# An encoder layer with experts on one core: rows of the first two experts taken from the residual by selection products

## What is computed

```
x = x + concat(a, b) @ w_out                      # residual after attention
t = rmsnorm(x, ffn_norm)
gl = t @ router_group + bias                       # 4 groups, the best is taken
el = t @ router_expert + bias                      # 8 experts in it, the best two are taken
out = sum over experts e: gates[:, e] * ((silu(t @ w_gate[e]) * (t @ w_up[e])) @ w_down[e])
y = rmsnorm(x + out, final_norm)
```

## Time and profile before

| | us |
|---|---|
| runs, median of 3 | 815.48 (814.65 to 816.72) |
| the profiled execution | 814.7 |
| its span, first to last instruction | 812.9 |
| mean granted clock of TensorE | 0.963 of full |
| TensorE busy | 711.2 (87%) |
| VectorE, ScalarE, GpSimd busy | 322.4, 214.0, 201.1 |
| hardware queue, software queue | 138.20 MB, 15.75 MB |

### The profile page before, as it was taken

The page is one execution under the profiler, slowest core; times in us unless marked ns, Lnnn a source line. Parts: engine busy times, 40 slices in busy tenths (PEclk is TensorE's granted clock), DMA queues, the critical chain, the costliest instruction groups (busy, mean ns, idle before and its releaser), DMA issues. The chain is left out here.

```text
span 812.9 us, 12172 instructions
## 1 busy us (share of the span) xinstructions
PE 711.2 (87%) x3978; PEld 399.4 (49%) x3979; DVE 322.4 (40%) x900; ACT 214.0 (26%) x575; POOL 201.1 (25%) x478
## 2 busy tenths in 40 slices
PE   6899999999988999989999965999997899999910
PEld 3455544444355666665555544555443445555500
DVE  3863121110088888881555561211111112111138
ACT  2433210011177777771211111111110111111123
POOL 1224232220024231132001223532232334342110
PEclk9999999999999999999999986999999999999975
DMA  8703002000140000000891168999999979999856
GB/s 299 295 1 104 0 1 103 1 0 1 35 178 1 1 1 1 2 2 0 344 418 69 76 238 307 303 336 378 396 343 386 355 258 365 407 374 394 356 224 254
DMA packets 40823, 154.64 MB, mean 190 GB/s; under 512 B 9642, under 2 KB 10794, under 8 KB 31936
## 3 DMA queue, kind: packets, MB, share of 16 engines
q1 hardware_dynamic: 33120, 138.20, 45.2%
q0 software_dynamic: 7648, 15.75, 5.8%
HBM read 142.29 MB, written 20.03 MB: 200 GB/s over the span
## 5 line engine op out<-in xcount | busy, mean ns | idle before, releaser
L1397 PE MATMUL banks<-arena 128*128 128x512 f32 (+1 forms) x384 | 163.4, 579 | 10.2 <-DMA arena<-w_in 8.0
L1662 PE MATMUL banks<-arena 128*64 128x256 f32 x1280 | 150.2, 388 | 10.6 <-DVE arena L1343 6.3
L1662 PEld LDWEIGHTS banks<-arena 128*64 128x64 f32 x1280 | 92.2, 139 | 59.4 <-issue 11.7
L1397 PEld LDWEIGHTS banks<-arena 128*128 128x128 f32 x384 | 72.1, 193 | 85.6 <-issue 77.9
L1553 PE MATMUL banks<-arena 128*128 128x512 f32 x192 | 86.4, 598 | 1.1 <-DVE arena L1162 1.1
L1672 PE MATMUL banks<-arena 128*64 128x512 f32 x320 | 77.4, 605 | 3.5 <-DVE arena L1347 3.1
L1118 DVE TENSOR_REDUCE arena<-banks 128x1 f32<-128x512 f32 (+1 forms) x96 | 55.3, 599 | 49.3 <-PE banks L1469 41.9
L904 ACT ACTIVATE arena<-banks,arena 128x512 f32<-128x512 f32 (+1 forms) x96 | 58.2, 611 | 43.4 <-DVE arena L1121 20.7
L1329 DVE TENSOR_TENSOR arena<-arena,banks 128x128 f32<-128x128 f32 x32 | 9.2, 288 | 134.7 <-ACT arena L998 119.2
L1553 PEld LDWEIGHTS banks<-arena 128*128 128x128 f32 x192 | 35.1, 190 | 38.8 <-issue 37.5
L730 POOL DMA_INDIRECT pair_rows<-arena x40 | 40.4, 1009 | 34.9 <-POOL arena L728 27.9
(11 more groups left out here) (184 smaller groups left out, 858.0 us busy)
## 6 DMA issues: line engine op xcount, KB each, us to landing
arena<-w_gate SPq DMA_DIRECT2D x32, 1024.0 KB, 6.0
arena<-w_up SPq DMA_DIRECT2D x32, 1024.0 KB, 11.2
arena<-w_down SPq DMA_DIRECT2D x32, 1024.0 KB, 8.9
arena<-w_in SPq DMA_DIRECT2D x3, 2048.0 KB, 8.3
arena<-pair_rows SPq DMA_DIRECT2D x5, 1024.0 KB, 11.6
arena<-w_out SPq DMA_DIRECT2D x1, 4096.0 KB, 12.8
arena<-xT SPq DMA_DIRECT2D x6, 512.0 KB, 10.5
arena<-x SPq DMA_DIRECT2D x6, 512.0 KB, 10.9
```

Source lines behind the costliest of these rows:

```text
L1397: last = nc.tensor.matmul(bank(mm % 2)[:, 0:GROUP_COLS[g]], xgT[:, t, c, :], w[:, c, :], start=(c == 0), stop=(c == DC - 1))
L1662: last = nc.tensor.matmul(bank(b)[h * SLOTS:(h + 1) * SLOTS, 0:2 * P].rearrange("p (g n) -> p g n", g=2), x_eT[i][:, c, :], w[:, :, c, h * ...
```

## The change

For experts 0 and 1 the rows of the first 64 slots are no longer gathered. VectorE's `choose(t)` builds in each tile a selection matrix `select[:, e, t, :]` (128 tokens x 64 slots): the one-hot of the rank, times whether the token's mask is set for expert e, times the row's rms factor. TensorE's `choose(e, t)` multiplies the residual tile by it in 8 pieces (weights `x_tok[:, t, :]`, viewed as "n (p c) -> n c p"; 64 columns) and sums over the tiles in bank 4+e. VectorE's `chosen_rows(e)` multiplies the sum by the norm's gain (`gain_rows`, one more small load at the start) into `x_eT[e]`. GpSimd starts with the gather of expert 2. In SyncE's list expert 31's weights come ahead of the ids, and wait for `xeT_psum` 2, the sums of both experts. The masks keep two tiles instead of six (`m1_of`, `m2_of`, index `t % 2`) wherever they were used.

```
@@ -178,7 +178,7 @@
-        M0 = K0 + 1412
+        M0 = K0 + 1420
...
+        gain_rows = k.take(DC)
...
-        m1_all = m.take(NT * NE).rearrange("p (t e) -> p t e", t=NT)
+        m1_of = m.take(2 * NE).rearrange("p (t e) -> p t e", t=2)
...
+        share = m.take(4).rearrange("p (i e) -> p i e", i=2)
+        select = m.take(2 * NT * SLOTS).rearrange("p (e t n) -> p e t n", e=2, t=NT)
...
+                    sp.dma_start(gain_rows, A["ffn_norm"].rearrange("o (p c) -> (o p) c", c=DC)).then_inc(lam_loaded, 16)
...
@@ -557,15 +564,16 @@
             load_expert(0, 4)
             load_expert(0, 5)
             store_residual(NT - 1)
+            sp.wait_ge(x2_stored, NT * 16)
+            sp.wait_ge(h2_ready, NT)
+            sp.wait_ge(rms2_ready, NT)
+            sp.wait_ge(x2T_psum, 2 * NT)
+            sp.wait_ge(xeT_psum, 2)
+            load_expert(NGRP - 1, members(NGRP - 1)[-1])
             sp.wait_ge(ids_scattered, 2 * NT * 16)
             for h in range(2):
                 sp.dma_start(yids_sb[h * SLOTS:(h + 1) * SLOTS, NE:].rearrange("r (b e) -> r b e", e=NE),
                              ids_dram.rearrange("(b r e) o -> r b (e o)", b=NBLK, e=NE)[:, 1:, :]).then_inc(ids_loaded, 16)
-            sp.wait_ge(x2_stored, NT * 16)
-            sp.wait_ge(h2_ready, NT)
-            sp.wait_ge(rms2_ready, NT)
-            sp.wait_ge(x2T_psum, 2 * NT)
-            load_expert(NGRP - 1, members(NGRP - 1)[-1])
             with sp.Fori(1, NGRP - 1) as g:
                 for s in range(RING):
                     load_expert(g, s)
...
@@ -781,10 +789,10 @@
                             scatter(YX, (more + 1) * NE + e, e_yid, c)
                 return words
-            gather_main(0, 0)
-            gather_main(0, 1)
+            pool.sem_inc(id_ready, 2)
+            gather_main(0, 2)
             note_pairs(NT - 1)
-            for s in range(2, AHEAD):
+            for s in range(3, AHEAD):
                 gather_main(0, s)
             pool.wait_ge(counts_ready, 1)
...
@@ -1244,10 +1252,25 @@
                     dve.tensor_scalar(onehot[:, i, :], const("iota_slot"), rank_f[:, i:i + 1], None,
                                       ALU.is_equal).then_inc(onehot_ready, 1)
+            def choose(t):
+                for i, mask in enumerate((m1_of, m2_of)):
+                    dve.tensor_scalar(share[:, i, :], mask[:, t % 2, 0:2], rs[:, t:t + 1], None, ALU.mult).then_inc(dve_chain, 1)
+                    chain[0] += 1
+                dve.wait_ge(dve_chain, chain[0])
+                dve.wait_ge(onehot_ready, 2 * t + 2)
+                for e in range(2):
+                    dve.tensor_scalar(select[:, e, t, :], onehot[:, 0, 0:SLOTS], share[:, 0, e:e + 1], None, ALU.mult).then_inc(dve_chain, 1)
+                    chain[0] += 1
+                dve.wait_ge(dve_chain, chain[0])
+                for e in range(2):
+                    dve.scalar_tensor_tensor(select[:, e, t, :], onehot[:, 1, 0:SLOTS], share[:, 1, e:e + 1], select[:, e, t, :],
+                                             ALU.mult, ALU.add).then_inc(select_ready, 1)
...
@@ -1320,6 +1344,12 @@
                 link(dve.reciprocal(pair[:, 0, :], nw[:, 0:NT]))
                 link(dve.tensor_tensor(pair[:, 1, :], pair[:, 0, :], second, ALU.mult))
+            def chosen_rows(e):
+                dve.wait_ge(xeT_psum, e + 1)
+                dve.tensor_tensor(x_eT[e], bank(4 + e).rearrange("p (c n) -> p c n", c=DC),
+                                  gain_rows.unsqueeze(2).to_broadcast([P, DC, SLOTS]), ALU.mult).then_inc(xeT_ready, 1)
             def dve_group(g):
...
@@ -1327,7 +1357,9 @@
                     n, before = extras(words, s)
                     dve.wait_ge(silu_done, e + 1)
                     dve.tensor_tensor(h_tok[s % 2], silu_t[s % 2], bank(1 + s % 2)[:, P:2 * P], ALU.mult).then_inc(h_ready, 1)
-                    if not isinstance(g, int) or e + 1 < NE:
+                    if isinstance(g, int) and e == 0:
+                        chosen_rows(1)
+                    elif not isinstance(g, int) or e + 1 < NE:
                         dve.wait_ge(xeT_psum, e + 2)
                         dve.tensor_copy(x_eT[(s + 1) % 2], bank(0).rearrange("p (c n) -> p c n", c=DC)).then_inc(xeT_ready, 1)
                     dve.wait_ge(hT_psum, e + 1)
...
@@ -1619,6 +1650,15 @@
                     last = nc.tensor.matmul(table, onehot[:, i, :], slot_of[:, i, :, :].rearrange("p w e -> p (w e)"),
                                             start=(t == 0 and i == 0), stop=(t == NT - 1 and i == 1))
                 last.then_inc(id_psum, 1)
+            def choose(e, t):
+                pe.wait_ge(select_ready, 2 * t + 2)
+                for c in range(DC):
+                    last = nc.tensor.matmul(bank(4 + e)[:, c * SLOTS:(c + 1) * SLOTS],
+                                            x_tok[:, t, :].rearrange("n (p c) -> n c p", c=DC)[:, c, :], select[:, e, t, :],
+                                            start=(t == 0 and c == 0), stop=(t == NT - 1 and c == DC - 1))
+                return last
             pe.wait_ge(ones_ready, 1)
...
@@ -1638,12 +1678,19 @@
             x2_transpose(NT - 1, 1)
             router(NT - 1, 0)
             router(NT - 1, 1)
+            for t in range(4):
+                choose(0, t)
             rank(NT - 1)
             counts = bank(1)[:, 0:NE]
             nc.tensor.matmul(counts, ones, macc[:, NT - 2, :], start=True, stop=False)
-            nc.tensor.matmul(counts, ones, m1_all[:, NT - 1, :], start=False, stop=False)
-            nc.tensor.matmul(counts, ones, m2_all[:, NT - 1, :], start=False, stop=True).then_inc(counts_psum, 1)
+            nc.tensor.matmul(counts, ones, m1_of[:, (NT - 1) % 2, :], start=False, stop=False)
+            nc.tensor.matmul(counts, ones, m2_of[:, (NT - 1) % 2, :], start=False, stop=True).then_inc(counts_psum, 1)
+            choose(0, NT - 2)
+            choose(1, 0)
             place(NT - 1)
+            for t in (1, 2):
+                choose(1, t)
+            choose(0, NT - 1).then_inc(xeT_psum, 1)
             def rows_transpose(b, i, chunks):
...
@@ -1691,8 +1738,12 @@
                     first = isinstance(g, int) and e == 0
                     pe.wait_ge(xeT_ready, e + 1)
                     gate_up(1 + s % 2, s % 2, weights(g, s)).then_inc(gu_done, 1)
-                    if not isinstance(g, int) or e + 1 < NE:
-                        await_count(rows_in[(s + 1) % RING], 16 * (g + (s + 1) // RING + 1))
+                    if isinstance(g, int) and e == 0:
+                        for t in range(3, NT):
+                            last = choose(1, t)
+                        last.then_inc(xeT_psum, 1)
+                    elif not isinstance(g, int) or e + 1 < NE:
+                        await_count(rows_in[(s + 1) % RING], 16 * (g + (s + 1) // RING + ((s + 1) % RING >= 2)))
                         rows_transpose(0, (s + 1) % RING, range(DC)).then_inc(xeT_psum, 1)
...
@@ -1725,8 +1776,6 @@
                 down(4 + s % 2, h_T[0], weights(g, s % RING)).then_inc(down_done, 1)
             pe.sem_inc(e_xeT_psum, 1)
-            pe.wait_ge(rows_in[0], 16)
-            rows_transpose(0, 0, range(DC)).then_inc(xeT_psum, 1)
             pe.wait_ge(counts_ready, 1)
             pe_group(0)
             with pe.Fori(1, NGRP - 1) as g:
...
```

More of the change, by code:

```diff
@@ L272, in build @@
         gain_ffn = m.take(D)
-        m1_all = m.take(NT * NE).rearrange("p (t e) -> p t e", t=NT)
-        m2_all = m.take(NT * NE).rearrange("p (t e) -> p t e", t=NT)
+        m1_of = m.take(2 * NE).rearrange("p (t e) -> p t e", t=2)
+        m2_of = m.take(2 * NE).rearrange("p (t e) -> p t e", t=2)
         macc = m.take(NT * NE).rearrange("p (t e) -> p t e", t=NT)
@@ L277, in build @@
         ones = m.take(P)
-        logit = m.take(NT * (NG + NE)).rearrange("p (t e) -> p t e", t=NT)
-        top = m.take(1)
-        max_g, max_1, max_2 = (m.take(NT) for _ in range(3))
         rank_f = m.take(2)
@@ L287, in build @@
         junk_c = m.take(256).bitcast(bf16)
+        logit = m.take(NT * (NG + NE)).rearrange("p (t e) -> p t e", t=NT)
+        top = m.take(1)
+        max_g, max_1, max_2 = (m.take(NT) for _ in range(3))
+        share = m.take(4).rearrange("p (i e) -> p i e", i=2)
+        select = m.take(2 * NT * SLOTS).rearrange("p (e t n) -> p e t n", e=2, t=NT)
+        m = Area(M0 + 3 * D, M0 + 4 * D)
         cnt = m.take(NE)
@@ L387, in build @@
         id_psum = sem("id_psum")
+        select_ready = sem("select_ready")
         slots_ready = sem("slots_ready")
@@ L1069, in _ @@
                 if i == 8:
-                    dve.wait_ge(lam_loaded, 6 * 16)
+                    dve.wait_ge(lam_loaded, 7 * 16)
                     for j in range(2):
@@ L1211, in route @@
                 first_max(key, masked, const("rev_e"), max1)
-                dve.tensor_scalar(m1_all[:, t, :], key, top, None, ALU.is_equal).then_inc(masks, 1)
```

(13 more changed lines are left out.)

20 lines of the change are left out of this document (10 added, 10 removed).

## The result

The changed kernel takes **856.92 us** (median of 4 runs, 854.75 to 858.33) against 815.45 beside it: a ratio of 1.051 (95% interval 1.0485 to 1.0534), 41.5 us slower. Slower was forecast, at 823.0; the time is 34 us above that and 12 above the range's end. The profiled execution has a span of 855.1 us, so it is set against the 812.9 of before.

What follows compares the result with a forecast made beforehand. TensorE and DMA both bound the expert stage, after a hole at 480 to 500 us. Expert 2 starting 8.5 us late, less 1.0 given back, adds 7.5 to 814.7: 822.2, median 823.0; range 817 to 845.

Steps and rivals of the forecast that it cites:

- wait for the ids: Before expert 2, VectorE waits for ids landing at about 516.8; expert 2 starts at 518.7 instead of 510.17, 8.5 us late.
- the sum: Whole kernel: expert stage ends 8.5 - 1.0 = 7.5 us later, so 822.2 us profiled and 823.0 median; chance 0.42.
- strided weights: Rival: choose's weight loads in steps of 8 words cost extra time, total 836, 844 or 851.6 us; chance 0.37.
- The rival's upper bound, 851.6: Strided weights at VectorE's whole 2.02 ns per element: 0.259 us per load, 4.14 us a choose, twelve adding 28.6 us.
- The clock: Through 480 to 500 us the granted clock stays at 1.0 instead of falling to 0.50, gaining 1.9 us at expert 0.
- 0.11 us for a contiguous product: Each instruction of a choose on TensorE takes 0.11 us, so a choose of 16 takes 1.76 us.
- the request "moved ahead": The last expert's weights, waiting for the chooses, are requested at 504.8 instead of 497.97, 6.8 us later.
- the ids queue behind 3 MB: In SyncE's queue the id reads wait behind 3.15 MB of weights landing at 514.8; ids there at about 516.8.
- the stall of VectorE: Inside expert 0's turn, VectorE stands some 11 us before its two operations on the ids.
- The doubt about giving back: After expert 2, waits total only 6.9 us; 1 us given back, 0 to 3 possible; rival of waits made up, 0.13.
- Faster: Rival: choose spacing below about 0.09 us and ids landing within 4 us of the request, 810 us total; chance 0.05.

Runs made afterwards that it cites:

- e2: Changed kernel with the selection products' weights read in contiguous words instead of a step of 8 words; output of experts 0 and 1 differs: 828.46 us, ratio 1.017.
- e7: e6 with the selection weights read in a step of 8 words again, and weights and gain in the order of before: 825.57 us, ratio 1.011.
- e6: e5 with only expert 0 built by selection products and expert 1's rows gathered again: 811.96 us, ratio 0.996; run again 813.38 us.
- e5: Changed kernel with the edits of e1 and e2, plus w_gate, w_up and gain of experts 0 and 1 loaded in matching order: 821.97 us, ratio 1.007.
- e1: Changed kernel with the two id reads ahead of the last expert's weights in SyncE's list again: 848.51 us, ratio 1.040.
- e8: e6 with the last expert's weight loads issued from ScalarE's queue, SyncE's queue keeping the ids: 817.95 us, ratio 1.003; profiled again 816.86 us.

## Why the prediction was wrong

Place by place, for the profiled execution (the forecast of each from the prediction's steps):

| stretch | forecast us | measured us | over | from |
|---|---|---|---|---|
| router's end to expert 0 | 495.6 | 517.2 | 21.6 | 1.5 later start; 144 x 0.13 = 18.7; ranks, counts, table at half clock 1.6 |
| expert 0 to 1 | 9.8 | 17.5 | 7.7 | 48 products, 6.4; gate and up at half clock 1.3 |
| expert 1 to 2 | 13.3 | 14.3 | 1.0 | wait for the ids, as forecast |
| expert 2 to 31 | 257.0 | 261.7 | 4.7 | half clock at expert 2, 2.5; nothing given back |

Together 35.0, and the span is 855.1 against 820.4 in the sum, 34.7.

**The step that failed** is "The forecast takes none of it, because VectorE's row has two inputs in steps and a weight load has one". The term "strided weights" was taken as 0 and is 25 us (e2 against the changed kernel; 12 to 14 for half as many products, e7 against e6). I had the right row and the right rule beside me, named the case as a rival with 0.37, and argued the price away with a difference that no row tested. The rival's upper bound, 851.6, was 5 us short although its 0.259 us per load was too dear, and my range stopped at 845, below it. With the measured 0.24 the same sum gives 848; what lay above is, by the table, the later start (1.5), the half clock (5.4, below) and longer waits: 1.0 for the ids and 2.2 behind expert 2, where I had 1.0 given back.

**The clock** was forecast as staying at 1.00, because TensorE would not be idle. It fell to 0.50 with TensorE busy in every microsecond of the records around the fall. With contiguous chooses (e2, e5) it stayed at 1.00 through the same stretch. Its own cost is bounded by the rows: the strided products are no slower for it (below), so it shows in what lies between, 1.6 + 1.3 + 2.8 (expert 1, 6.51 against 3.67, within a stretch where the ids were awaited anyway) + 2.5. Some 5 us of it are on the path. The last 2.5, expert 2's products, are not the step's: TensorE had stood waiting for the ids, and e2 has them too (6.19).

**Right**: the number of instructions and their places; 0.11 us for a contiguous product, and the starts of experts 0 and 1, which e2 shows within 0.5 us of the sum (expert 2 came 2.0 late); that the request "moved ahead" comes later and that the ids queue behind 3 MB (10.4 us to landing; e1 gives 8.2 us of cost, 2.5 of it the clock; I had 6.9 at expert 2, 518.7 against 511.8, less 1.0); the stall of VectorE (12.5 us, forecast 11). The doubt about giving back was right in kind and too hopeful in size: from expert 2 to 31 the kernels with late ids took 261.7 and, in e2, 263.1 us against before's 258.0; with the ids early, in e1, it was 257.9, so nothing was given back there either. DMA had stood empty meanwhile (11 GB/s, above, and 10 in e2 from 494 to 504), so the stream of weights was as late as TensorE; that this is why nothing was made up is a reading, not tested.

**Faster** needed, I wrote, a spacing under 0.09 us. e6 found another way to it that I had not priced: half of the change. Expert 0's chooses fill a hole that waits for DMA; those of expert 1 stand on the path of an engine that has no hole there, 5.6 us for a wait that did not exist.

## What to carry to other kernels

A transposed view costs nothing to write and, as fp32 weights read in steps of 4 or 8 words, doubled the time of every load with its 64 columns here: before a strided view goes into a loop, look for one row of any engine that reads in that step, and put its price per element into the sum, not beside it. Here the same freedom was to be had in the layout of the other operand, through a load that runs anyway. Work that is put into a hole is worth the hole only: count what stands there once it is full, and where the second helping goes. And a request that is moved ahead in a queue is not earlier unless what it waits for is; what now stands behind it is later, on a DMA queue as on an engine (e8).

## What the runs showed of the hardware

- The price of a weight load with a step of 4 or 8 words does not depend on the granted clock (table above); with 1 or 2 words it does. In the changed kernel the clock came back to 1.00 between 520 and 526 us, and the products went on at the same pace; in two microseconds each, on either side:

```profile
524.00:526.00 2.00, 2.00 (x10) 2.00 (x10) 0.00 (x0) 0.00 (x0) 0.00 (x0) 1.00 0.00 0
528.00:530.00 2.00, 2.00 (x10) 2.00 (x9) 0.00 (x0) 0.00 (x0) 0.00 (x0) 0.50 0.00 0
```

- A TensorE that the records call busy throughout can be granted half the clock. It happened early in the chooses of each profile with a step of 4 or 8 words, and a second time at about 527 in the three of them that also chose expert 1's rows and had come back to 1.00. It happened at about 489 in the one with 2 words, and in one of the seven with contiguous weights, the first of e8, with the same instructions up to there as e6. That one execution shows the contiguous product at half clock, 48 in 9.13 us, against 5.55 in e6:

```profile
478.46 9.13 PE L1668 MATMUL banks<-arena 128*128 128x64 f32 x48
```

So the step is not the only cause of the fall; what decides it in an execution is not settled by these runs.
- A read of 88 KB in small packets takes 3.8 us with nothing in front, 10.4 us behind 3 MB that were requested 1.3 us before it in the same queue. Another queue did not save it: 12.0 us where the 3 MB went to ScalarE's queue 0.3 us before it (second profile of e8), 3.8 where they went there 1.6 us after it (the first).
